# Eight scan steps written out in sequence, in place of loops on the engines

## What is computed

```python
def step(S, inp):
    r_t, w_t, k_t, v_t, kk_t, b_t = inp
    sa = -jnp.einsum("bhvk,bhk->bhv", S, kk_t)
    S = S * w_t[:, :, None, :] + sa[..., None] * b_t[:, :, None, :] + v_t[..., None] * k_t[:, :, None, :]
    return S, jnp.einsum("bhvk,bhk->bhv", S, r_t)
...
s_fwd_c, y_fwd_c = rwkv_scan(zero_state, fc, 0, reverse=False)
s_bwd_c, y_bwd_c = rwkv_scan(zero_state, fc, 1, reverse=True)
_, y_fwd_x = rwkv_scan(s_fwd_c, fx, 0, reverse=False)
_, y_bwd_x = rwkv_scan(s_bwd_c, fx, 1, reverse=True)
```

## Time and profile before

| | |
|---|---|
| median of 3 runs | 2599.65 us (2588.39, 2599.65, 2602.11) |
| the profiled execution: its time | 2587.97 us |
| its span | 2586.1 us |
| mean granted TensorE clock | 0.932 of full |
| busy: PE, DVE, ACT, POOL | 87%, 52%, 36%, 14% |
| the scan in layer 0 | about 260 to 540 us |
| the scan in layer 1 | about 1731 to 2010 us |

### The profile page before, as it was taken

One profiled execution on the slowest core, in us unless ns is written; L12 is line 12 of the kernel. 1 busy time (PEld: TensorE's weight loads), 2 busy tenths in 40 slices (PEclk: granted clock), 3 DMA queues, 4 the chain that ended last, 5 costly groups with the idle time before them and its releaser, 6 DMA issues. The chain is left out here.

```text
span 2586.1 us, 47543 instructions
## 1 busy us (share of the span) xinstructions
PE 2244.5 (87%) x19733; PEld 1706.8 (66%) x19733; DVE 1341.7 (52%) x2028; ACT 919.7 (36%) x1597; POOL 364.2 (14%) x461
## 2 busy tenths in 40 slices
PE   6896788879998999889999987958888798997998
PEld 2383677743256888668887834827777534997998
DVE  5747767762373333353332266487766535454544
ACT  4623444423042222232222165234433223343442
POOL 1102433300300001010000011033323021010000
PEclk9998999989699999899999988979999878998999
DMA  8630000020011333113232285100000301463543
GB/s 290 210 138 1 2 0 2 0 109 19 0 34 59 98 94 102 65 66 98 98 98 98 82 282 199 61 1 1 0 1 1 126 1 37 143 190 114 179 164 131
DMA packets 157292, 219.44 MB, mean 85 GB/s; under 512 B 6814, under 2 KB 123768, under 8 KB 156128
## 3 DMA queue, kind: packets, MB, share of 16 engines
q1 hardware_dynamic: 155648, 215.74, 25.0%
q0 software_dynamic: 1504, 1.71, 0.2%
HBM read 208.00 MB, written 9.44 MB: 84 GB/s over the span
## 5 line engine op out<-in xcount | busy, mean ns | idle before, releaser
L332 DVE TENSOR_TENSOR W_low<-RING,W_high 128x1024 fp32r<-128x1024 f32 x364 | 444.9, 1231 | 483.8 <-ACT W_high L329 483.0
L329 ACT ACTIVATE W_high<-RING 128x1024 fp32r<-128x1024 f32 x364 | 380.0, 1053 | 662.7 <-PE BANK L370 614.2
L368 PE MATMUL BANK<-H_high,W_high 128*128 128x512 f32 (+2 forms) x1472 | 526.9, 358 | 76.9 <-ACT H_high L584 35.5
L369 PE MATMUL BANK<-H_low,W_high 128*128 128x512 f32 (+2 forms) x1472 | 520.4, 354 | 0.0
L370 PE MATMUL BANK<-H_high,W_low 128*128 128x512 f32 (+2 forms) x1472 | 520.0, 353 | 0.0
L368 PEld LDWEIGHTS BANK<-H_high,W_high 128*128 128x128 f32 (+1 forms) x1472 | 283.5, 193 | 131.5 <-issue 51.5
L370 PEld LDWEIGHTS BANK<-H_high,W_low 128*128 128x128 f32 (+1 forms) x1472 | 283.7, 193 | 38.3
L369 PEld LDWEIGHTS BANK<-H_low,W_high 128*128 128x128 f32 (+1 forms) x1472 | 284.3, 193 | 36.8 <-issue 1.1
L1160 PE MATMUL BANK<-RING,WORK 64*64 64x64 f32 x4096 | 170.9, 224 | 48.5 <-DVE RING L1098 31.7
L1160 PEld LDWEIGHTS BANK<-RING,WORK 64*64 64x64 f32 x4096 | 149.1, 139 | 61.7 <-issue 61.5
L973 POOL TENSOR_TENSOR WORK<-WORK,masks 128x256 f32<-128x256 f32 x160 | 120.3, 763 | 155.4 <-PE BANK L1160 151.8
(11 more groups left out here) (268 smaller groups left out, 3454.4 us busy)
## 6 DMA issues: line engine op xcount, KB each, us to landing
RING<-w_mod_dram SPq DMA_DIRECT2D x48, 1024.0 KB, 5.1
RING<-w_in_dram SPq DMA_DIRECT2D x46, 1024.0 KB, 5.3
RING<-w_ffn_in_dram SPq DMA_DIRECT2D x44, 1024.0 KB, 5.0
RING<-w_ffn_out_dram SPq DMA_DIRECT2D x22, 1024.0 KB, 4.8
RING<-w_out_dram SPq DMA_DIRECT2D x8, 1024.0 KB, 5.1
h_high<-H_high SPq DMA_DIRECT2D x2, 2048.0 KB, 6.4
h_low<-H_low SPq DMA_DIRECT2D x2, 2048.0 KB, 11.9
H_high<-h_high SPq DMA_DIRECT2D x2, 2048.0 KB, 10.8
```

What stands on the lines that cost most here:

```text
L329: high_ready.mark(nc.scalar.activation(self.part(0, c), self.raw(c), ACT.Copy))
L332: low_ready.mark(nc.vector.tensor_tensor(self.part(1, c), self.raw(c), self.part(0, c).bitcast(FP32), ALU.subtract))
L368: nc.tensor.matmul(out, w[0], x[0], start=start, stop=False)
L369: nc.tensor.matmul(out, w[0], x[1], start=False, stop=False)
```

## The change

The loops go: `run` calls `step` eight times with numbers, so that offsets and the values waited for are constants, and all `hold` calls with their three semaphores go too. Nothing else changes: the same operations, in the same order on each engine.

```diff
-    waits_passed = {e: ctx.enter_context(nc.semaphore(f"waits_passed_{e}")) for e in ("pe", "dve", "pool")}
-
-    def hold(eng, name="pe"):
-
-
-        eng.sem_inc(waits_passed[name], 1)
...
         def tokens(eng, d, i):
-            t = chunk_of(d, i)
-            return t if isinstance(i, int) else eng.snap(t, min_val=0, max_val=TOK - CHUNK)
+            return chunk_of(d, i)

         def run(eng, step):

-            for first, end, need_y in ((0, N, context_y), (N, STEPS - 1, True)):
-                Signal.trips = end - first
-                with eng.Fori(first, end) as i:
-                    step(i, need_y, True)
-                Signal.trips = 1
-            step(STEPS - 1, True, False)
+            for i in range(STEPS):
+                step(i, context_y or i >= N, i < STEPS - 1)
...
                         for d in range(NDIR):
                             pe.wait_ge(*at_step(s_t[d], i, LEVELS, l))
                             pe.wait_ge(*at_step(s_lm[d], i, NL, l))
-                            hold(pe)
...
                         for d in range(NDIR):
                             pe.wait_ge(*at_step(s_x1_out[d], i, NL, l))
-                            hold(pe)
```

More of the change, by code:

```diff
@@ L954, in operands @@
                     pool.wait_ge(*at_step(s_exp, i, 2, d + 1))
-                    hold(pool, "pool")
                     s_ops[d].mark(nc.gpsimd.tensor_tensor(BK[d][:, :, 1], KD[d][:, :, bass.ds(t, CHUNK)], EXPS[d][:, 2], ALU.mult))
@@ L1059, in exponents @@
                     dve.wait_ge(*at_step(s_exp, i, 2))
-                    hold(dve, "dve")
                     nc.vector.tensor_tensor(EXPO[:, 0], whole, EXCL[1][:, :, at], ALU.subtract)
```

## The result

The change made the kernel slightly slower: median **2604.08 us** (2598.35 to 2610.67, 11 runs) against 2593.85 us (2586.65 to 2602.11, 11 runs) of the kernel before, a ratio of 1.004 with a 95% interval of 1.0025 to 1.0054. The forecast was 2590, a gain of 0.2%. The time lies in the stated range, but on the other side of the kernel before: 10 us slower instead of 4.5 faster.

The account below looks back on a forecast made before the run. The scan was taken as bound by hand-offs and DVE's run, no engine filling a step. -10.8 (loop steps) - 1.2 (last steps) + 7.5 (fresh code) = -4.5 us, from 2594.5 to 2590; range 2575 to 2607.

Parts of the forecast that it names:

- What is removed elsewhere: the holds on DVE and POOL ... so nothing: Scan: holds and register moves run ahead of instructions that wait longer for something else, so removing them gains nothing.
- What bounds the kernel: Scan step: no engine fills it; DVE's unbroken run of 13 us, then 21 us of single hand-offs.
- The hand-offs: Scan waits shrink once holds and register arithmetic go: 0.77 us a loop step, about 0.6 each last step, 12.0 us together.
- The fresh code: Ten scan steps now executed once from fresh instructions, 0.75 us each: +7.5 us, between +1 and +17.
- rival 1: Ten written-out scan steps: fresh code costs nothing, all 12.0 us of gain stay, 2582.5 us; chance 0.20.
- The jumps: Loop branches back to the next scan pass: no gap shows there, so removing them was priced at nothing.
- rival 4: Scan steps' clock stays high throughout or falls in as many more: 2580 or 2600 us; chance 0.12, mostly the better side.
- Rival 2: Scan hand-offs: waits don't shrink or something else is late; gain 5 us or less, 2597 us; chance 0.18.
- Rival 3: Written-out scan steps: PE's instruction supply becomes the bound, +19 us, 2614 us; chance 0.12.
- the signs of being wrong: Changed scan: steps of 33.9 us without pauses, steps over 35 with several each, or DVE pausing in its run.
- a pause of DVE between L1125 and L1087: DVE's run in a scan step: a pause there would count in full and show the forecast wrong.
- theory C: Scan, named after the result: PE's longer idle time during DVE's run lowers its clock; more PE work should gain 3 to 12.

Follow-up runs that it names:

- e1: The change with one hold put back, on GpSimd ahead of its decay copy; 2585.73 us, ratio 0.9972 to the kernel before.
- e3: The kernel before with its steps written out and all holds kept; 2602.09 us, ratio 1.0041 to the kernel before.
- e6: The change with PE's ten holds and GpSimd's holds put back, none on DVE; 2603.23 us, ratio 1.0036 to the kernel before.
- e5: The change with GpSimd's decay copy and product moved behind its masks of levels 2 and 3; 2576.64 us, ratio 0.9937 to the kernel before.
- e4: The kernel before, loops and holds kept, with GpSimd's decay copy and product moved behind its level-1 masks; 2622.37 us, ratio 1.0113.
- e7: The kernel before, loops and holds kept, with GpSimd's decay work moved behind its masks of levels 2 and 3; 2582.53 us, ratio 0.9959.
- e2: The change with GpSimd's decay copy and product moved behind its level-1 masks; 2604.7 us, ratio 1.0049 to the kernel before.
- e10: The change with two holds in a row put back on GpSimd ahead of its decay copy; 2585.67 us, ratio 0.9985 to the kernel before.
- e9: e5 with PE's transposes of the values at level 1 done three times; 2570.45 us, ratio 0.9925 to the kernel before.
- e8: The change with PE's transposes of the values at level 1 done three times; 2603.06 us, ratio 1.0028 to the kernel before.

## Why the prediction was wrong

**The step that failed** is the one under "What is removed elsewhere: the holds on DVE and POOL ... so nothing". I asked whether GpSimd bounds a step, and it doesn't. But the hold doesn't run ahead of the wait, as that sentence has it: it follows the wait, so GpSimd starts later by its length (0.19 us behind DVE in e1, 0.06 in the change). I should have asked what an earlier GpSimd runs beside. The term put at nothing measured +10.2 us in part A of the profile, and e1 prices this hold alone at 18 us of the change's time, the clock included.

**What bounds the kernel:** right. DVE's run and the hand-offs are the two parts of a step, and both moved on their own.

**The hand-offs:** the mechanism was right, the size too high. 0.77 us a step was forecast; B at full clock went from 21.59 to 21.09, 0.50. (e1's whole step, 33.20 against 33.89, gained 0.69, but 0.17 of that is in A.) Steps without y gained 0.66, the last ones 0.94 where 0.6 was forecast: over the 14 steps 8.4 for 10.4. The wait is 0.10, not 0.05: in e1 L1106 starts at 347.14, its first ends 0.64 later, and PE starts at 347.88.

**The fresh code:** +7.5 us was forecast, and the change has nothing of it. The four fresh steps that I averaged all had holds on PE. The term described the kernel that keeps them, and was too large even for it (e3's pauses sum to 3.8 us more than those of before, e6's to 4.7). For the change rival 1 was right on this point. I had taken a difference of fresh and repeated passes as the price of fresh code, without asking what else these passes had in common.

**The jumps:** priced at nothing, and nothing in the runs speaks against it.

**The clock (rival 4):** the wrong sign. In the kernel before five of the 14 steps have a low clock that shows in B; in the changed kernel all 14 have. I took the better side as likelier.

**Rival 2** had it that the waits don't shrink or that something else is late instead. They shrank, though by two thirds of what was forecast. What was late is in part A, which it didn't name.

**Rival 3**, slower by late instructions, had the sign of the result but not its cause. Nothing of it is in the changed trace. Of the signs of being wrong the last came nearest, a pause of DVE between L1125 and L1087: there is no pause, but one copy is 1.6 us longer.

The sum over the 14 steps, profiled execution against profiled execution, worked out from A and B of each step (B at full clock is 21.59, 19.50 without y and 20.95 in the last step before; 21.09, 18.84 and 20.01 now, taken from e1 and e5, whose text for PE is the same, since no step of the change is at full clock; what lies above is pause or clock):

| | us |
|---|---|
| A: 172.3 to 182.4, DVE behind GpSimd | +10.2 |
| B at full clock: the hand-offs | -8.4 |
| B: pauses inside groups, 2.9 to none | -2.9 |
| B: low clock, 6.0 to 17.6 | +11.6 |
| sum: 475.9 to 486.4 | +10.5 |
| outside these steps (2110.2 to 2115.4) | +5.2 |
| span: 2586.1 to 2601.8 | +15.7 |

Of the 5.2 us, 2.1 lie ahead of the first of these steps (302.43 against 300.30), 1.7 between the two scans and 1.4 behind them; these weren't followed. The profiled execution of before was among its fastest, so the medians differ by 10.2, not 15.7.

**What stays open** is the clock. What lies over full clock in B, pauses taken off, from one profile each:

| | A, mean | over full clock in B |
|---|---|---|
| loops: before | 12.3 | 6.0 |
| loops: e4 | 13.3 | 21 |
| loops: e7 | 11.8 | about 6.5 |
| written out with PE's holds: e3, e6 | 12.4, 12.2 | about 7, 12 |
| written out, no holds on PE: change, e2 | 13.0 | 17.6, 17.0 |
| the same: e1, e10 | 12.2 | 12.7, 13.8 |
| the same: e5, e9 | 11.6, 11.2 | 12.7, 11.3 |

So the low clock isn't tied to the written-out form: e4 has most of it, and differs from before only in GpSimd's place. Where A is longer, by the meeting with GpSimd, there is more of it: about 5 of the 11.6 us went with the meeting (change to e1). That goes the way of theory C. But e3 and e6 differ by 5 at nearly the same A, and e8 and e9, made to test theory C, don't bear it out: with more work for PE, e8 has as much low clock as the change, and e9 has 8 such steps, as e5. Why e1 has twice as much as the kernel before isn't shown.

## What to carry to other kernels

Before taking a wait or a delay off an engine that isn't the bottleneck, list what it will then run beside, and look above all for GpSimd beside DVE's copies and its operations with both sources in SBUF: a start that moved by 0.2 us cost 0.8 us a step here. When two passes of the same code differ, find what the slow ones share besides being slow before pricing it; here "fresh code" was "fresh code behind holds". And a delay can be worth keeping: put such work where DVE reads PSUM or waits, which here was worth 0.6% where the change itself had lost 0.4%.

## What the runs showed of the hardware

- DVE's copy of 64 x 512 took 2.01 us for 0.41 when GpSimd's product started within 0.01 us of it, and it waited through the next instruction of GpSimd too (change, 305.69). With GpSimd's instruction ahead of that product 0.13 us later, the same copy wasn't delayed, and the product was, 1.32 for 1.03 (e1, 338.27). In both the product starts level with the copy: the start times don't tell who will wait.
- DVE instructions with both sources in SBUF took 1.07 and 1.57 us for 0.42 and 0.69 beside GpSimd (e2), those with a PSUM source didn't change.
- PE behind DVE: 0.28 us with a register wait and a hold, 0.19 with constants and a hold, 0.10 with the wait on the matmul (e1).
- Ten fresh steps of PE code without holds: no pause over 0.05 us inside a group, in seven traces. With holds on PE, written out (e3, e6): six and seven pauses of 0.5 to 1.7 us, each ending 1.2 to 1.5 us behind the end of a 16 KB packet of instructions.
